# Expert weights in transfers of 2 MB where two half places fall free together

## The reference, cut to what matters

```python
def grouped_moe(h, router_w, router_bias, w1, w3, w2):
    ...                                   # gates: two experts per token, of one group of four
    for e in range(N_EXPERTS):            # 16 experts, D_MODEL 1024, D_EXPERT 512
        a = jax.nn.silu(t @ w1[e]) * (t @ w3[e])
        y = y + gates[:, e:e + 1] * (a @ w2[e])
```

## Time and profile before

| | |
|---|---|
| median of 3 runs | 1050.93 us (1049.51 to 1054.65) |
| the profiled execution, its time | 1051.37 us |
| its span, first to last instruction | 1049.6 us |
| TensorE matmul busy | 1001.3 us (95%) |
| VectorE busy | 564.4 us (54%) |
| queue of SyncE, its packets' share of 16 DMA engines | 79.4%, 323.56 MB |
| mean granted TensorE clock | 0.989 |
| half blocks of the experts issued | 192 of 1 MB |

### The profile page before, as it was taken

How to read it: one execution, slowest core, us unless ns; L and a number is a source line. 1 busy time by engine, 2 the same in 40 slices (tenths; PEclk the granted TensorE clock), 3 DMA queues, 4 the chain that set the end, 5 groups by cost and what they waited for, 6 DMA issues and landing times.

```text
span 1049.6 us, 18343 instructions
## 1 busy us (share of the span) xinstructions
PE 1001.3 (95%) x7711; PEld 603.9 (58%) x7711; DVE 564.4 (54%) x1192; ACT 188.5 (18%) x395; POOL 40.0 (4%) x82
## 2 busy tenths in 40 slices
PE   6999999999999999999999999999999999999784
PEld 3688667667785444443358866765878534444321
DVE  4578795868786223352235779672758622333112
ACT  4031001211233121011131110132123311110102
POOL 2100100010000000000010010001000000000000
PEclk9999999999999999999999999999999999999997
DMA  9998946297976999999999894627875599999991
GB/s 310 385 383 299 309 162 242 71 315 287 407 300 219 421 387 420 421 420 421 421 397 367 287 328 163 222 71 273 312 277 213 199 421 421 421 419 421 421 419 76
DMA packets 91851, 333.88 MB, mean 318 GB/s; under 512 B 5724, under 2 KB 6027, under 8 KB 66933
## 3 DMA queue, kind: packets, MB, share of 16 engines
q1 hardware_dynamic: 87937, 323.56, 79.4%
q0 software_dynamic: 2944, 7.12, 2.3%
q10 hardware_dynamic: 884, 1.97, 0.6%
HBM read 329.47 MB, written 1.05 MB: 315 GB/s over the span
## 4 chain that ended last, share of the span: by engine, by line
PE 83%; DVE 9%; DMA 3%; issue 2%; ACT 1%; SPq 1%; DVEq 0%; ACTq 0%
PE bank L822 80%; DMA ring<-in_moe_w_dram 2%; SPq L721 1%; PE bank L1335 1%; PE bank L1111 1%; DVE wide L2004 0%; DVE area L2000 0%; DVE wide L1796 0%; PE bank L1164 0%; DVE x L2220 0%; PE bank L885 0%; DVE area L2219 0%; DVE area L2196 0%; DVE wide L2005 0%; DVE area L2003 0%
## 5 line engine op out<-in xcount | busy, mean ns | idle before, releaser
L822 PE MATMUL bank<-ring,hT 128*32 128x512 f32 (+3 forms) x1808 | 280.2, 548 | 4.9 <-DMA ring<-in_moe_w_dram 2.1
L822 PE MATMUL bank<-hT,ring 128*32 128x256 f32 (+1 forms) x2112 | 213.5, 381 | 0.7 <-DVE hT L1820 0.7
L822 PEld LDWEIGHTS bank<-ring,hT 128*32 128x32 f32 (+2 forms) x1808 | 119.8, 133 | 137.8 <-issue 132.5
L822 PEld LDWEIGHTS bank<-hT,ring 128*32 128x32 f32 (+1 forms) x2112 | 158.6, 132 | 53.3 <-issue 6.1
L822 PE MATMUL bank<-ring,area 128*32 128x512 f32 (+1 forms) x744 | 119.4, 571 | 0.9 <-ACT area L1670 0.9
L822 PE MATMUL bank<-area 32*64 32x64 f32 (+5 forms) x648 | 89.1, 363 | 0.0
L1796 DVE SCALAR_TENSOR_TENSOR area<-ring,wide,area 128x512 f32<-128x512 f32 x114 | 85.3, 748 | 2.7
L2428 DVE TENSOR_TENSOR area<-bank,area 128x512 f32<-128x512 f32 x14 | 9.7, 692 | 128.9 <-PE bank L822 128.9
L822 PE MATMUL bank<-wide,hT 128*32 128x512 f32 (+1 forms) x376 | 76.8, 584 | 1.4 <-DMA ring<-in_moe_w_dram 1.4
L822 PEld LDWEIGHTS bank<-ring,area 128*32 128x32 f32 (+1 forms) x744 | 43.8, 121 | 55.2 <-issue 50.1
L822 PEld LDWEIGHTS bank<-area 32*64 32x64 f32 (+4 forms) x648 | 37.9, 145 | 45.6 <-issue 44.4
(11 more groups left out here) (302 smaller groups left out, 1082.1 us busy)
## 6 DMA issues: line engine op xcount, KB each, us to landing
ring<-in_moe_w_dram SPq DMA_DIRECT2D x136, 1024.0 KB, 15.2
ring<-in_w_ada_dram SPq DMA_DIRECT2D x24, 2048.0 KB, 14.5
ring<-in_w_in_dram SPq DMA_DIRECT2D x24, 2048.0 KB, 12.3
wide<-in_moe_w_dram SPq DMA_DIRECT2D x32, 1024.0 KB, 12.9
cst<-in_moe_w_dram SPq DMA_DIRECT2D x13, 1024.0 KB, 13.2
area<-in_moe_w_dram SPq DMA_DIRECT2D x11, 1024.0 KB, 13.7
ring<-in_w_out_dram SPq DMA_DIRECT2D x4, 2048.0 KB, 8.6
ring<-in_w_br_h_dram SPq DMA_DIRECT2D x4, 1536.0 KB, 6.7
```

The source lines that it names most:

```text
L822: return pe.matmul(dst, lhsT, rhs, start=start, stop=stop, skip_group_check=True)
```

## The change

In steps 1 to 5 of each layer ("two to six" counted from one), a load of half 0 looks at the two places that have been free longest. If one of them is a half whose neighbour is also among the oldest (among the first two or three), the whole block goes into the pair: one transfer of 2 MB, which waits for both former contents, is told by one semaphore, and takes the position of half 0 in the queue. Half 1 is then left out of the queue. Both halves have the same landing value, so TensorE's wait for half 0 becomes a wait for the whole block. Otherwise the half is loaded as before. Steps 0 and 6 and the mixer's weights are loaded as before. The arithmetic does not change.

```diff
+WHOLE_STEPS = range(1, 6)
...
+        pairs = ring + [wide[:, h * 8 * W:(h + 1) * 8 * W] for h in range(2)]
...
+        whole = set()
...
-                    u, old = free.pop(0)
-                    while (L, u) in LAST and b[0] > LAST[L, u]:
+                    if (L, b) in whole and half:
+                        continue
+                    free = [f for f in free if b[0] <= LAST.get((L, f[0]), STEPS)]
+                    near = [i for i in range(2) if free[i][0] < TABLE and free[i][0] ^ 1 in [f[0] for f in free[:i + 2]]]
+                    if half == 0 and b[0] in WHOLE_STEPS and near:
+                        u = free[near[0]][0] & ~1
+                        olds = [old for f, old in free if f in (u, u + 1)]
+                        free = [f for f in free if f[0] & ~1 != u]
+                        whole.add((L, b))
+                        for h in range(2):
+                            part = (L, kind, b, h)
+                            plan[part] = halves[u + h], u, landings[u] + 16, olds[:1] if olds[0] == olds[1] else olds
+                            free.append((u + h, part))
+                    else:
                         u, old = free.pop(0)
-                    plan[key] = halves[u], u, landings[u] + 16, [old]
-                    free.append((u, key))
+                        plan[key] = halves[u], u, landings[u] + 16, [old]
+                        free.append((u, key))
...
             for L, kind, b, half in loads:
+                if half and (L, b) in whole:
+                    continue
...
-                    part = slice(half * (NF if m == 2 else ND) // 2, (half + 1) * (NF if m == 2 else ND) // 2)
+                    rows = (NF if m == 2 else ND) // 2
+                    part = slice(half * rows, (half + 1) * rows)
+                    if (L, b) in whole:
+                        dst, part = pairs[u // 2], slice(0, 2 * rows)
```

## The result

| | before | after |
|---|---|---|
| median of 8 runs | 1052.24 us (1049.51 to 1054.65) | 1059.42 us (1055.97 to 1064.36) |
| ratio, 95% interval | | 1.0064 (1.0043 to 1.0086) |
| the profiled execution, its time | 1051.37 us | 1059.48 us |
| its span | 1049.6 us | 1057.7 us |

A forecast was written before the change was run, and what follows sets the result against it. TensorE was taken to bound the kernel, except layer 1's last two steps, paced by weight transfers. +2.1 (layer 0) + 0.9 - 1.05 (layer 1) = +1.95 on the 1050.93 us median gave 1052.9 us, range 1049 to 1056.5.

The forecast's parts named there:

- The one place named in layer 0: Step 5's `up` for m1 in layer 0: TensorE idles 1 to 3 us until a ring transfer lands.
- +0.9: Layer 1, steps 5 and 6: whole-block waits start step 6 2.1 us later, but its 1.17 us gap goes.
- 1.05: Layer 1: 21 whole blocks each save 0.05 us of stream, so landings come 1.05 us earlier; bounds 0 and 1.8.
- the joined waits: Layer 1: waiting for both places costs nothing; tightest at step 3's w1 of expert 1, 0.7 us in hand.
- the lateness of the stream in layer 0: Layer 0, at w2 of step 3: stream late by 0.7 us, at least 0.3 and at most 1.2.
- The late start: Layer 0, step 1, w3 of expert 1: first whole block waits for a second half, issued 3.5 us later.
- The 2.3: Layer 0, step 3's first release: 2.3 us of stream were unused at 281 GB/s, absorbing part of the 3.5 us delay.
- +2.1: Layer 0, step 5, m1: `up` starts 2.1 us later, waiting for the last whole block; bounds +1.4 and +3.0.
- such a fall may come or go: Experts' steps: a clock fall to 1.2 GHz may appear or vanish as idle time moves, 1.7 us each way.
- c: Stream time saved per whole 2 MB block against two halves: 0.05 us, between nothing and 0.085.
- large rows: Rival, both layers: 16 KB rows run at 387 GB/s, a block takes 5.42 us for 4.98, total 1067; chance 0.07.
- a lead for each transfer: Rival: each transfer pays 2.5 us unhidden, so merging gains up to 9.7 us, time 1041; chance 0.03.

The follow-up runs named there:

- e1: Kernel after, with whole blocks in layer 0 only; 1059.22 us, ratio 1.0050 to the kernel before.
- e3: Kernel after, but the three w3 blocks (m1) of step 5 in layer 0 loaded in halves; 1055.34 us, ratio 1.0030.
- e4: Kernel before, but the three w3 blocks (m1) of step 5 in layer 0 loaded whole; 1053.60 us, ratio 1.0002.
- again: The kernel after, unchanged, timed and profiled a second time; 1057.78 us, ratio 1.0055 to the kernel before.
- e2: Kernel after, with whole blocks in layer 1 only; 1054.01 us, ratio 1.0005 to the kernel before.
- e9: Kernel after, but in layer 0 steps 1 and 2 and step 5's w3 loaded in halves; 1055.66 us, ratio 1.0027.
- e6: Kernel after, with whole blocks only in layer 0 and only in steps 2 to 5; 1057.42 us, ratio 1.0044.
- e8: Kernel after with whole blocks in layer 0 only, plus 10 unused matmuls before layer 0's `up(5, 1)`; 1056.88 us, ratio 1.0037.
- before's second run: The kernel before, unchanged, run once more for its profile; 1055.17 us.
- e10: Kernel after, with only 13 far-ahead blocks whole, all in layer 1's steps 3 to 5; 1051.78 us, ratio 0.9992.
- e7: Kernel after with whole blocks in layer 0 only, plus 20 unused matmuls before layer 0's `up(5, 1)`; 1059.96 us, ratio 1.0061.
- e5: Whole blocks' pairs, joined waits and order in layer 0 only, each pair as two 1 MB transfers with own semaphores; 1056.27 us, ratio 1.0019.

## Why the prediction was wrong

**Right: where.** The one place named in layer 0, the idle before `up(5, 1)` ended by a ring transfer, is where the loss is; e1, e3 and e4 show it. Layer 1 came out near the forecast, +0.9 - 1.05 = -0.15 against +0.1 (after), -0.6 (again) and +0.4 (e2). That is partly luck: the saving and the joined waits were both larger than I had them, as told below, and the same 23 blocks gave -1.1 in e3 and +2.3 in e9.

**The step that failed first: the lateness of the stream in layer 0, mis-sized.** The late start was right: the whole block (1, 1, 1) went out at 336.71 after, and the single half at 330.12 before, 3.1 of that the start's shift; so 3.5 (SyncE's issues in order of time, before and after):

```profile
330.12 0.33 SPq L721 DMA_DIRECT2D cst<-in_moe_w_dram  x1
```

```profile
336.71 0.33 SPq L741 DMA_DIRECT2D wide<-in_moe_w_dram  x1
```

The stretch at step 3's first release was to give 2.3 of it back. In landings the stream is 3.9 late at step 2's end (55.0 against 51.1), and 2.4 at the end of step 3's w1 (70.63 against 68.27), so it gave back 1.5. At w2 of step 3, where I took 0.7 with a bound of 1.2, it is 90.2 against 88.2, **2.0 late** (1.5 to 2.4 in the three other traces with the same blocks there: after again, e1, e3). The 2.3 was the mean rate over all 16 DMA engines, 281 GB/s. But a transfer has landed when the slowest engine has, and the slowest had idled less: before, (3, 0, 0) landed 3.59 us after the transfer ahead of it where 2.48 is the pace, 1.1 us of idle. The semaphore's first and sixteenth increments for that transfer ahead lie 1.80 us apart. The Trainium skill (DMA: Bandwidth & Descriptors, section Why a DMA increments its semaphore by 16 and not by 1) says that a transfer's engines finish independently, each adding one; this trace agrees, with the 1.80 us. The mean over the engines told how many bytes were missing, not when the last engine ran dry.

With 2.0 in place of 0.7, less 8 x 0.08 for the rate, the block lands 1.4 later than its half 1 did before (159.4 against 158.0), and `up(5, 1)` starts at 159.5 of the layer's count against 156.3: +3.2 where I had +2.1, just past the bound of +3.0. e6 and e9 add that the lateness does not hang on the one wait that I had worked it out from.

**The step left out: the clock behind the new idle.** I wrote that "such a fall may come or go, 1.7 us each way", had one in the high end, and put none into the sum, though the earlier trace rows showed one behind an idle time of 3.29 us and I was forecasting a new idle in a place with nothing behind it to hide a slow half. It cost 1.7 (8.77 - 7.07; e8 has it gone). The idle itself was longer than the start's delay, since the old fall at 439 us was gone in this execution and TensorE came 1.6 us earlier: 3.2 + 1.6 = 4.8, read 4.72. That gain was worth nothing, as before's second run shows (207.8).

**The sum, mended.** 3.2 + 1.7 = 4.9 for layer 0, which is what was read, and +0.1 for layer 1: +5.0, for a forecast of +1.95. The sets give about the same or more: the means lie 5.4 (after, again) and 5.8 us (e1) above before's, 6.8 in the first set. The profiled layers build up the same way: 208.0 before, 209.5 with the whole wait alone (e4), 211.4 with the late stream too (e8, its filling matmuls in place of the idle), 213.3 with the clock's fall (e1). This comes from one profile each; the medians agree in order but, at e4 and e3, not in size.

**The rest of the miss is the base.** I added to the median of 3 runs, 1050.93; of 8 it is 1052.24, and before's runs scatter from 1049.5 to 1055.6. 1052.24 + 5.0 = 1057.2; the remaining 2.2 to 1059.42 is within that scatter, and the second median of the kernel after was 1057.78.

**The rate: mis-sized a little, low.** I took c = 0.05, bound 0.085. Three whole blocks issued from 431.30 on, 0.49 us apart, in a full queue (us to landing, the kernel after):

```profile
ring<-in_moe_w_dram SPq DMA_DIRECT2D x1, 2048.0 KB, 16.8
...
ring<-in_moe_w_dram SPq DMA_DIRECT2D x1, 2048.0 KB, 21.2
...
ring<-in_moe_w_dram SPq DMA_DIRECT2D x1, 2048.0 KB, 25.6
```

4.4 + 0.49 = 4.89 us apart, against 2 x 2.49 = 4.98 of halves: c = 0.08 to 0.09. The same stretch by packets, 12 us of each kernel, before and then after:

```profile
DMA packets 694, 5.05 MB, mean 421 GB/s; under 512 B 79, under 2 KB 79, under 8 KB 79
```

```profile
DMA packets 357, 5.10 MB, mean 425 GB/s; under 512 B 39, under 2 KB 39, under 8 KB 39
```

Half the packets, 1% more bytes. So large rows are not slower, and a lead for each transfer isn't there to save; both rivals fell. The Trainium skill (DMA: Bandwidth & Descriptors, section Anatomy of one DMA — SWDGE (gpsimd) path, not the section Bandwidth that I named) fits about 2.0 us of fixed cost to each transfer, for transfers that GpSimd issues; here SyncE issues them. By an estimate from that page's figure 43 transfers fewer would save 86 us of queue time; in the full queue here a merged pair saved 0.08 to 0.09 us.

**The joined waits in layer 1.** I held that the stream does not break. It does, at the place that I had named as the tightest, w1 of expert 1 in step 3. In the kernel after that block is issued at 883.50 and the transfer ahead lands at 885.97, so 2.47 us later and not 3.2: even by the slowest engine my 0.7 us in hand are gone. The first of the sixteen increments of the transfer ahead comes at 884.35 already, so the fastest engines run dry first, before the lead of 2.5 us is over. The block's first increment follows 5.85 us after that one, for 4.89, and its landing 5.25 us after the landing ahead. All five traces with this block whole show the step (first increments 5.84 to 6.04 us apart, landings 5.25 to 6.49), and e10, which loads it in halves, does not. So this join costs 0.4 to 1.6 us. Two more landings in step 3 of the kernel after come late, 5.80 and 5.69 us after the one before, and neither repeats in its second trace. The 5.80 is no join: the block was issued 3.9 us before the fastest engine was free, and fifteen of the sixteen increments keep the pace. The 5.69 is one in part: that block was issued 1.7 us before the fastest engine was free, and its first increment came 5.21 us after the one ahead; the rest stays open. By step 5's last landing the stream is 1.4 us earlier than before (168.2 against 169.6), and that with the kernel before having a jump of 1.5 us on the way (at 952.27). So the steps had eaten most of what 21 x 0.08 = 1.7 us of rate give. e9's layer 1, 205.8, is the longest of all; the clock stood low for 10.2 us in it, behind idle times of 3.43 and 3.16 us, against 3.4 us before.

**Step 5 of layer 1** went by the steps I gave, moved by sizes. m0 waited 1.69 (forecast 2 to 3), m1's half 0 0.26 (almost none), m1's half 1 3.78 (3.8) with the clock's fall behind it. `down(5)` waited 0.28 where I had 1.5 to 3.5: the fall took 6.50 - 3.64 = 2.9 us of that wait's place. Step 6's first `up` still lost 1.06 before its half 1; I had that gone. The landing that it waited for, at 1015.17, came 4.17 us after the one before, for 2.49. So half 1 starts 179.9 us into the layer's count, against 179.6 before.

## What to carry to other kernels

Merging two transfers saves what the packets cost (here 0.08 us in 4.98), and takes away the first half's early landing: before merging, compare TensorE's lead at each place with the delay of the first half, here 5.0 us by order, 2.1 by the late stream and 2.1 by the single semaphore. Where a new idle is in sight, put not only the wait into the sum but the clock behind it. And work out a stream's slack from landings, not from the mean rate of all DMA engines, and take the base from more than three runs if they scatter by more than the effect.

## What the runs showed of the hardware

- The clock fell behind all of TensorE's idle times from 3.16 us up in the experts' steps (3.16 and 3.43 in e9, 3.29 before, 3.78 and 4.72 after, 4.60 in e6, 5.17 in e1, 5.19 after again, among others) and behind none of those from 1.0 to 2.13 us (2.03 in e3 among them). In between it went both ways: it fell behind 2.50 and 2.58 (e2), 2.75 (e7), 2.84 (e8) and 3.04 (before, again), all in layer 1, and not behind 2.72 (e4), 2.84 (e1), 2.89 (e5), 2.99 (e6) or, in layer 0, the two of 3.06 (e4, e5). And the fall at 439 us of the earlier trace rows, like one at 439.5 in e9, has only 0.44 us of idle before it, which the other twelve traces have as well, without a fall. So the length of one idle time does not decide it. The fall in layer 0's `up(5, 1)` cost 1.6 to 1.7 us. The stretch behind the 4.72 and that behind e4's 3.06:

```profile
492.00:498.00 6.00, 5.29 (x36) 1.91 (x40) 0.00 (x0) 0.00 (x0) 0.00 (x0) 0.72 1.01 421
```

```profile
491.00:498.00 7.00, 6.79 (x64) 2.39 (x64) 0.00 (x0) 0.00 (x0) 0.00 (x0) 1.00 1.00 417
```

- It also fell at 30 us, in the mixer, with 0.74 us idle right before it in the kernel before; e3 has the same 0.74 there and no fall. Over the profiled executions it lasted not at all (2), 3.4 us (4) or 10.2 us (8), and the start of layer 0's count goes with it, from 328.8 to 334.5 us.
- The rate rose with the piece per packet, 387 GB/s at 2 KB, 421 at 8 KB, 425 at 16 KB, and is nearly flat by 8 KB.
- Landings jump by 1 to 1.7 us now and then in every kernel (before at about 836 and 952 us, after at 844 and 1015). Packets of the instruction queue lie beside them: in the kernel after one of 16 KB starts at 898.15 and takes 0.99 us, and in the next transfer one of the sixteen increments is some 1.6 us late while the others keep the pace. Whether they are the cause was not tried, and stays open.
- The sixteen DMA engines drift apart in a full queue. In the kernel before, the first and the last increment of one transfer lie 0.5 us apart at 832.44, where the queue had been empty, 2.1 at 848.92, and 3.6 at 952.27.
